# The first loads in halves, and the first norm's square sums behind the first dense products, in a single-core chain of three transformer blocks

## The chip, the cores and the metric

The kernel runs on one core of a Trainium2 chip. The metric is the device time in microseconds (us) of one execution; smaller is better. A core has TensorE (PE: matrix products; its weight loads are shown as PEld and overlap the products), ScalarE (ACT), VectorE (DVE), GpSimd (POOL) and SyncE (SP), which here only issues transfers. Each engine runs its own program in order, and the programs meet at semaphores.

## The reference

Three blocks are run one after the other on 256 tokens of 1024 numbers. Only the first lines of the first block matter here:

```python
h = rmsnorm(x, attn_norm_g)            # x * rsqrt(mean(x*x) + 1e-6) * g
m = rmsnorm(mem, mem_norm_g)
proj = h @ w_in                        # 8704 columns: da_q, da_k, da_v, wa_q, ...
da_q, da_k, da_v, wa_q, wa_k, wa_v, xa_q, gates = jnp.split(proj, offsets, axis=-1)
```

Three attentions (differential, windowed, and to a memory), their gates, an output product, a mixture of 16 experts, and then the second and third blocks follow. None of them is changed.

## The kernel before

**Layout.** Activations lie feature by feature: `self.x` is 128 partitions by 8 groups `f` of features by 256 tokens. The inputs come so from memory (`xT`, 1024 KB). `vecs` holds the gains, and the first columns of `consts` an identity matrix and a matrix of ones over 1024.

**Products in three parts.** For accuracy every dense product takes both operands as a rounded half and a rest: a = hi + lo. ScalarE writes `hi` (`a_hi`, line 582), VectorE writes `lo = a - hi` (`v_lo`, line 593), and `t_three` (lines 620, 621, 622) issues three matmuls: hi·hi, hi·lo, lo·hi. A 1024 KB load of weights holds 256 output columns of all 1024 rows; it is rounded in two pieces, `h = 0` (rows 0 to 511) and `h = 1`, each 128x1024. `t_fm` works through one such load as 24 matmuls of 256 token columns for `h = 0` and 24 for `h = 1`, and it yields after each of the two.

**The first projection.** The first stage is `mix`. The projection `daq` (4 loads, called c0 to c3 here, load numbers 0 to 3) doesn't wait for the norm: its right operand `xg` is x times the gain, in two halves (`gained` on ScalarE, line 1965; `gained_lo` on VectorE, line 1493), and the factor 1/sqrt(mean square) is applied to the product afterwards, in `q_out` (line 1508). That factor, `RSTD`, comes from this sequence: ScalarE squares x (`a_square`, line 953, four pieces), TensorE sums them over the features with the matrix of ones (`t_rms`, line 936, eight plain float32 products, shown as 16 matmul records), ScalarE takes the root (`a_sd`, line 971), VectorE the reciprocal (`v_rstd`, line 976). The same sequence, with squares added up first by GpSimd, is run for `mem` some 30 us later. The normed x proper (`v_normed`, lines 983 and 989; `a_normed`, line 966) is wanted only by the second projection, `dak`.

**Order of the programs.** There is no planner for this part: each engine's order is written out by hand.
- TensorE (`t_mix`): wait for all first inputs; `t_rms("n1")`; c0 to c3 of `daq`; then `dak`, with `t_rms("mem")` inside it.
- ScalarE (`a_mix`): four squares; gained(0); hi of load 0, h=0; gained(1); hi of load 0, h=1; gained(2); gained(3); the load of the root's table (line 804); `a_sd("n1")`; then hi of load 1, both pieces, then hi of load 2, and so on.
- VectorE (`v_mix`): gained_lo(0); lo of load 0, h=0; gained_lo(1); lo of load 0, h=1; gained_lo(2), (3); `v_rstd("n1")`; then lo of load 1, both pieces; `q_out` of c0; pieces of the normed x; lo of load 2; and so on.
- SyncE (`sync`): x (line 522), then the weight loads in order (line 544), with `mem` behind load 1 (line 546) and small tables behind load 3. ScalarE's own queue carries `vecs` and the first `consts`. Four slots hold weights, so load 4 waits until both pieces of load 0 are rounded.

The PSUM banks for `daq` are two in turn, so c2 needs `q_out` of c0 done.

Of the kernel before, what the change touches and what calls it, by code (L numbers as in the profile page):

```python
# [231 lines left out]
class Program:  # L232
    def __init__(self, nc, A, out, ctx):
# [24 lines left out]
        self.side = Landed(sem("side_landed")), Landed(sem("side2_landed"))  # L258
        self.router_in, self.tables_in = Landed(sem("router_landed")), Landed(sem("second_tables_landed"))
# [16 lines left out]
        self.first_all, self.rest_all = (self.first_in, 48), (self.rest_in, 16 * 9)  # L276
# [243 lines left out]
    def sync(self, e):  # L520
        S, A = Met(), self.A
        e.dma_start(self.B(2), A["xT"]).then_inc(*self.first_in.one())
        for q in self.order:
# [19 lines left out]
            for r, (view, src) in enumerate(load.parts):  # L543
                e.dma_start(view(base), src).then_inc(*(self.row_in[r] if q == self.tail else self.landed[load.slot]).one())
# [32 lines left out]
    def a_hi(self, e, i, h):  # L577
        load, step = self.loads[i], self.loads[i].n // 2
        c = slice(h * step, h * step + step)
        for w in self.Aw.new(load.value, *self.pair_free(i, h)):  # L580
            e.wait_ge(*w)
        e.activation(self.WH[load.pair][:, c], self.base(i)[:, c], ACT.Copy).then_inc(*self.act.inc(("hi", i, h)))  # L582
# [5 lines left out]
    def v_lo(self, e, i, h):  # L588
        load, step = self.loads[i], self.loads[i].n // 2
        c = slice(h * step, h * step + step)  # L590
        for w in self.Vw.new(load.value, self.act.val(("hi", i, h))):
# [678 lines left out]
    def t_mix(self, e):  # L1270
        DB, KB, OB = Ring(0, 1), Ring(2, 3, 4, 5, 6, 7, 0, 1), Ring(6, 7)
        H, mp, act = self.H, self.mp, self.act
        for w in self.Tw.new(self.first_all):
            e.wait_ge(*w)
        self.t_rms(e, "n1", self.B(9), KB)
        run(self.t_proj(e, "daq", 4, self.xg, self.halves("xg"), DB, self.by_dve("daq")))
# [87 lines left out]
    def a_mix(self, e):  # L1364
        act = self.act
        for j in range(4):
            self.a_square(e, "n1", self.x, self.B(9), j, [self.first_all])
        gained = lambda j: self.a_gained_hi(e, "xg", self.x, self.xg[0], lambda f: self.V("attn_norm_g", f), j, [])
        gained(0)
        self.a_hi(e, 0, 0)  # L1370
        gained(1)
        self.a_hi(e, 0, 1)
        gained(2)
        gained(3)
        self.a_sqrt_table(e)
# [107 lines left out]
    def v_mix(self, e):  # L1483
# [3 lines left out]
        for w in self.Vw.new(self.first_all):  # L1487
            e.wait_ge(*w)
        def gained_lo(j):
            for f in (2 * j, 2 * j + 1):  # L1490
                for w in self.Vw.new(self.act.val(("xg", "h", f))):
# [5 lines left out]
        gained_lo(1)  # L1497
        self.v_lo(e, 0, 1)
        self.v_next = 1
        gained_lo(2)  # L1500
# [156 lines left out]
    def g_mix(self, e):  # L1657
        for w in self.Gw.new(self.first_all):
# [1863 lines left out]
    def begin(self, dry):  # L3522
# [3 lines left out]
        for landed in (*self.landed, *self.row_in, *self.side, self.first_in, self.rest_in, self.late_in, self.rows_in, self.router_in, self.tables_in):  # L3526
# [102 lines left out]
```

## Time and the profile before

| | |
|---|---|
| time, median of 3 runs | 2701.94 us (2701.65 to 2703.44) |
| the profiled execution's own time | 2701.89 us |
| span in its profile | 2699.2 us |
| TensorE busy | 2302.2 us, 85% of the span |
| VectorE busy | 1255.6 us, 47% |
| ScalarE busy | 932.8 us, 35% |
| GpSimd busy | 54.8 us, 2% |
| moved by the DMA queues | 695.45 MB, mean 258 GB/s |

The span runs from the first to the last record of the profile; the execution's own time is 2.7 us more. Busy time is the union of an engine's instructions. The profile is of one execution.

### The profile page before, as it was taken

The numbers are of one execution on the slowest core, as the hardware profiler recorded it, in microseconds if no ns is written. First come the engines' busy times: TensorE is split into PE (matmuls) and PEld (weight loads), VectorE is DVE, ScalarE is ACT, GpSimd is POOL, SyncE is SP. The second block draws the span as 40 slices with busy tenths as digits, with TensorE's granted clock in tenths as the row PEclk, the third lists the DMA queues.
The fourth block names the chain that finished last, engine by engine and source line by source line (L and its number), as shares of the span: only waits on it lengthen the run. The fifth ranks groups of instructions, "written<-read, shape, count | busy, mean of one in ns | idle before, by whom it ended". The sixth has DMA issues, their size and how long they took to land.

```text
span 2699.2 us, 37912 instructions
## 1 busy us (share of the span) xinstructions
PE 2302.2 (85%) x16606; PEld 1676.6 (62%) x16606; DVE 1255.6 (47%) x1778; ACT 932.8 (35%) x1528; POOL 54.8 (2%) x40
## 2 busy tenths in 40 slices
PE   8999999556566556666699999999999999998998
PEld 8897785112122111212378888888888888887887
DVE  6567663001000000101287865577656556866655
ACT  6556551000000000000255654455443543743443
POOL 0000000000000000000100000000000000003000
PEclk9999999888878887878899999999999999999999
DMA  7543479999999999999934365665554654313652
GB/s 249 172 156 110 140 281 389 430 432 431 431 430 431 430 431 430 432 431 432 347 110 157 105 224 187 203 234 201 190 187 172 203 184 145 120 60 127 203 187 93
DMA packets 236549, 695.45 MB, mean 258 GB/s; under 512 B 10304, under 2 KB 189888, under 8 KB 221408
## 3 DMA queue, kind: packets, MB, share of 16 engines
q1 hardware_dynamic: 234080, 679.15, 65.9%
q0 software_dynamic: 2016, 13.67, 1.4%
q8 instruction: 130, 2.13, 0.3%
q14 instruction: 35, 0.29, 0.0%
q10 hardware_dynamic: 288, 0.22, 0.0%
HBM read 691.96 MB, written 1.05 MB: 257 GB/s over the span
## 4 chain that ended last, share of the span: by engine, by line
PE 63%; DMA 28%; DVE 6%; ACT 2%; issue 1%; SPq 0%; ACTq 0%; DVEq 0%
DMA af<-in_w_exp_up 18%; PE ps L620 16%; PE ps L622 16%; PE ps L621 16%; DMA af<-in_w_exp_down 9%; PE ps L1765 4%; PE ps L1802 2%; DVE ar L593 2%; PE ps L2771 1%; PE ps L2335 1%; ACT af L1124 1%; DVE af L1163 1%; PE ps L936 1%; PE ps L1232 1%; DVE sm L1202 0%
## 5 line engine op out<-in xcount | busy, mean ns | idle before, releaser
L620 PE MATMUL ps<-ar 128*128 128x512 f32 (+2 forms) x2648 | 926.2, 350 | 7.6 <-DVE ar L3486 2.1
L621 PE MATMUL ps<-ar 128*128 128x512 f32 (+2 forms) x2648 | 906.7, 342 | 0.8 <-issue 0.8
L622 PE MATMUL ps<-ar 128*128 128x512 f32 (+2 forms) x2648 | 907.0, 343 | 0.0
L593 DVE TENSOR_TENSOR ar<-af,ar 128x1024 fp32r<-128x1024 f32 x516 | 609.4, 1229 | 216.4 <-ACT ar L582 216.3
L582 ACT ACTIVATE ar<-af 128x1024 fp32r<-128x1024 f32 x516 | 511.8, 1048 | 130.9 <-PE ps L622 114.2
L620 PEld LDWEIGHTS ps<-ar 128*128 128x128 f32 x2648 | 502.1, 190 | 81.3 <-issue 9.6
L622 PEld LDWEIGHTS ps<-ar 128*128 128x128 f32 x2648 | 502.0, 190 | 59.2
L621 PEld LDWEIGHTS ps<-ar 128*128 128x128 f32 x2648 | 502.7, 190 | 56.4 <-issue 1.5
L1765 PE MATMUL ps<-af 128*32 128x512 f32 x2048 | 322.0, 787 | 230.3 <-DMA af<-in_w_exp_up 153.7
L1765 PEld LDWEIGHTS ps<-af 128*32 128x32 f32 x2048 | 74.9, 139 | 468.6 <-issue 189.3
L1939 DVE TENSOR_TENSOR af<-af,ps 128x512 f32<-128x512 f32 x16 | 11.0, 688 | 534.1 <-ACT af L1849 534.1
L1802 PE MATMUL ps<-af,cst 128*32 128x512 f32 x1024 | 155.6, 754 | 87.9 <-DMA af<-in_w_exp_down 76.4
L1849 ACT ACTIVATE af<-ps 128x512 f32<-128x512 f32 x16 | 9.6, 597 | 582.4 <-PE ps L1765 582.4
L1654 DVE TENSOR_TENSOR af<-ps,af 128x512 f32<-128x512 f32 x76 | 48.1, 684 | 262.9 <-PE ps L1814 249.0
L1802 PEld LDWEIGHTS ps<-af,cst 128*32 128x32 f32 x1024 | 38.8, 133 | 191.5 <-DMA af<-in_w_exp_down 101.1
L1856 ACT ACTIVATE cst<-ps 128x512 f32<-128x512 f32 x16 | 9.6, 597 | 271.1 <-PE ps L1802 271.1
L2392 DVE TENSOR_TENSOR af<-af,ps 128x256 f32<-128x256 f32 x66 | 27.5, 421 | 124.7 <-ACT af L2363 124.7
L2363 ACT ACTIVATE af<-ps 128x256 f32<-128x256 f32 x66 | 25.0, 384 | 135.1 <-PE ps L622 135.0
L1124 ACT ACTIVATE af<-af,sm 128x256 f32<-128x256 f32 (+1 forms) x136 | 64.0, 474 | 21.0 <-DVE sm L1210 13.2
L2354 ACT ACTIVATE ar<-ps 128x512 fp32r<-128x512 f32 x44 | 26.3, 599 | 80.5 <-PE ps L2335 80.5
L1112 ACT ACTIVATE af<-ps 128x384 f32<-128x384 f32 (+1 forms) x60 | 29.4, 536 | 52.8 <-PE ps L1076 52.8
L2379 DVE TENSOR_TENSOR ar<-ps,ar 128x512 fp32r<-128x512 f32 x44 | 30.4, 692 | 26.5 <-ACT ar L2354 26.3
(324 smaller groups left out, 1655.3 us busy)
## 6 DMA issues: line engine op xcount, KB each, us to landing
af<-in_w_exp_gate SPq DMA_DIRECT2D x30, 4096.0 KB, 33.5
af<-in_w_exp_up SPq DMA_DIRECT2D x30, 4096.0 KB, 33.4
af<-in_w_exp_down SPq DMA_DIRECT2D x28, 4096.0 KB, 33.6
af<-in_ffn_w_in SPq DMA_DIRECT2D x88, 1024.0 KB, 5.7
af<-in_ffn_w_out SPq DMA_DIRECT2D x44, 1024.0 KB, 5.2
af<-in_w_in SPq DMA_DIRECT2D x34, 1024.0 KB, 5.3
af<-in_sgu_w_in SPq DMA_DIRECT2D x16, 1024.0 KB, 6.9
af<-in_w_exp_down SPq DMA_DIRECT2D x7, 2048.0 KB, 12.0
```

Source lines behind the costliest of these rows:

```text
L582: e.activation(self.WH[load.pair][:, c], self.base(i)[:, c], ACT.Copy).then_inc(*self.act.inc(("hi", i, h)))
L593: e.tensor_tensor(self.WL[load.pair][:, c], self.base(i)[:, c], f_(self.WH[load.pair][:, c]), ALU.subtract).then_inc(*self.dve.inc(("lo", ...
L620: e.matmul(o, lh, rh, start=start, stop=False, skip_group_check=True)
L621: e.matmul(o, lh, rl, start=False, stop=False, skip_group_check=True)
L622: return e.matmul(o, ll, rh, start=False, stop=stop, skip_group_check=True)
L1112: e.activation(self.PT()[:, m, 0:at[1].stop], self.ps[:, 4 + m, 0:at[1].stop], ACT.Copy).then_inc(*self.act.inc((name, "p", i, m)))
L1124: e.activation(d, d, ACT.Exp, bias=st[:, g:g + 1], accum_out=st[:, 4 + g:5 + g]).then_inc(*self.act.inc((name, "e", i, g)))
L1654: e.tensor_tensor(d, it(self.bank((name, c))), d, ALU.add).then_inc(*self.dve.inc(("out", name, c)))
L1765: t = e.matmul(ps[32 * j:32 * j + 32, bb, :], XE[:, k, c:c + 32], k_(self.base(q), rows)[:, r, 512 * j:512 * j + 512], start=k == 0, stop= ...
L1802: t = e.matmul(ps[o:o + 32, b, :], self.AT_[x % 2][:, at:at + 32], k_(self.base(q), rows)[:, r, 512 * c:512 * c + 512], start=j == 0 and r ...
L2379: e.tensor_tensor(lo[:, v, :], it(self.bank((name, "t", c))), f_(hi[:, v, :]), ALU.subtract).then_inc(*dve.inc((name, "l", c)))
L2392: e.tensor_tensor(G, G, up, ALU.mult).then_inc(*done)
```

## The change

What is loaded stays the same, in more pieces. The first 1024 columns of x (feature groups 0 to 3), then the first half of load 0 (rows 0 to 511), then the rest of x, then the rest of load 0 are issued as four transfers of 512 KB in place of two of 1024 KB, each with a semaphore of its own or, for the last, the slot's. The instructions that round the first piece wait for the first halves only.

ScalarE's order becomes gained(0), hi(0, h=0), gained(1), gained(2), hi(0, h=1), gained(3), and then the four squares, the table, `a_sd`. VectorE's becomes gained_lo(0), lo(0, h=0), gained_lo(1), gained_lo(2), lo(0, h=1), gained_lo(3), and then, as before, `v_rstd`, lo of load 1. TensorE runs both halves of c0 first, then `t_rms("n1")`, then c1 to c3. No arithmetic changes.

```diff
-        self.first_all, self.rest_all = (self.first_in, 48), (self.rest_in, 16 * 9)
+        self.tables_all, self.half_all = (self.first_in, 32), ((self.x_half_in, 16), (self.w_half_in, 16))
+        self.first_all, self.rest_all = (self.tables_all, (self.x_rest_in, 16)), (self.rest_in, 16 * 9)
...
-        e.dma_start(self.B(2), A["xT"]).then_inc(*self.first_in.one())
+        e.dma_start(self.B(2)[:, 0:1024], A["xT"][:, 0:1024]).then_inc(*self.x_half_in.one())
+        (view, src), place = self.loads[0].parts[0], self.base(0)
+        e.dma_start(view(place)[:, 0:4, :], src[:, 0:4, :]).then_inc(*self.w_half_in.one())
+        e.dma_start(self.B(2)[:, 1024:2048], A["xT"][:, 1024:2048]).then_inc(*self.x_rest_in.one())
...
             for r, (view, src) in enumerate(load.parts):
+                if q == 0:
+                    e.dma_start(view(base)[:, 4:8, :], src[:, 4:8, :]).then_inc(*self.landed[load.slot].one())
+                    continue
...
-        for w in self.Aw.new(load.value, *self.pair_free(i, h)):
+        for w in self.Aw.new(self.half_all[1] if i == 0 and h == 0 else load.value, *self.pair_free(i, h)):
...
-        for w in self.Vw.new(load.value, self.act.val(("hi", i, h))):
+        for w in self.Vw.new(self.half_all[1] if i == 0 and h == 0 else load.value, self.act.val(("hi", i, h))):
...
     def t_mix(self, e):
-        for w in self.Tw.new(self.first_all):
+        daq = self.t_proj(e, "daq", 4, self.xg, self.halves("xg"), DB, self.by_dve("daq"))
+        next(daq)
+        next(daq)
+        for w in self.Tw.new(*self.first_all):
             e.wait_ge(*w)
         self.t_rms(e, "n1", self.B(9), KB)
-        run(self.t_proj(e, "daq", 4, self.xg, self.halves("xg"), DB, self.by_dve("daq")))
+        run(daq)
...
     def a_mix(self, e):
-        for j in range(4):
-            self.a_square(e, "n1", self.x, self.B(9), j, [self.first_all])
-        gained = lambda j: self.a_gained_hi(e, "xg", self.x, self.xg[0], lambda f: self.V("attn_norm_g", f), j, [])
+        gained = lambda j: self.a_gained_hi(e, "xg", self.x, self.xg[0], lambda f: self.V("attn_norm_g", f), j,
+                                            [self.tables_all, self.half_all[0]] if j < 2 else self.first_all)
         gained(0)
         self.a_hi(e, 0, 0)
         gained(1)
+        gained(2)
         self.a_hi(e, 0, 1)
-        gained(2)
         gained(3)
+        for j in range(4):
+            self.a_square(e, "n1", self.x, self.B(9), j, self.first_all)
         self.a_sqrt_table(e)
         self.a_sd(e, "n1", 1e-6)
...
         gained_lo(0)
         self.v_lo(e, 0, 0)
         gained_lo(1)
+        gained_lo(2)
         self.v_lo(e, 0, 1)
         self.v_next = 1
-        gained_lo(2)
         gained_lo(3)
         self.v_rstd(e, "n1")
```

## Rows read from the trace of the kernel before

**Rows 1.** The page, busy time: engine, us, share of the span, instructions.

```profile
PE 2302.2 (85%) x16606; PEld 1676.6 (62%) x16606; DVE 1255.6 (47%) x1778; ACT 932.8 (35%) x1528; POOL 54.8 (2%) x40
```

**Rows 2.** Busy time by stretch: us and instructions by engine, granted clock, DMA share.

```profile
0.00:300.00 300.00, 286.81 (x1879) 249.97 (x1880) 197.79 (x304) 177.82 (x339) 4.11 (x7) 0.99 0.51 169
700.00:1300.00 600.00, 362.63 (x2528) 117.97 (x2532) 46.85 (x82) 13.14 (x22) 0.00 (x0) 0.81 1.00 431
```

**Rows 3.** SP's waits over the span: us in total, times, longest.

```profile
SPq L544 <- PE ps L1765: 438.3, 47, 15.6
```

**Rows 4.** The chain that ended last, in order of time: start us, us, what.

```profile
1.25 6.01 DMA cst<-in_consts
...
8.05 6.35 PE ps L936 x16
...
43.19 0.88 PE ps L936 x4
44.09 0.48 ACT sm L971
44.60 1.77 DVE sm L976
...
48.78 1.24 DVE ar L593
```

**Rows 5.** TensorE's timeline: first matmuls of c0 and c1; start us, us.

```profile
14.05 0.47 PE L620 MATMUL ps<-ar 128*128 128x256 f32 x1
...
19.98 0.28 PE L620 MATMUL ps<-ar 128*128 128x256 f32 x1
```

**Rows 6.** Line 936 in two windows: min/median/max ns, first and last start us.

```profile
L936 PE MATMUL ps<-af,cst x3: 634/634/634, 10.7 to 11.6; 128*128 128x256 f32 x3
...
L936 PE MATMUL ps<-af,cst x5: 379/454/634, 12.4 to 13.8; 128*128 128x256 f32 x5
```

**Rows 7.** ScalarE's timeline, in order of time.

```profile
7.28 2.19 ACT L953 ACTIVATE af<-af 128x512 f32<-128x512 f32 x4 [4.26 <-DMA cst<-in_consts]
9.37 0.89 ACT L1965 ACTIVATE ar<-af,vec 128x256 fp32r<-128x256 f32 x2
10.17 1.04 ACT L582 ACTIVATE ar<-af 128x1024 fp32r<-128x1024 f32 x1
11.11 0.89 ACT L1965 ACTIVATE ar<-af,vec 128x256 fp32r<-128x256 f32 x2
...
15.97 0.46 ACT L971 ACTIVATE sm<-ps,sm 128x256 f32<-128x256 f32 x1
```

**Rows 8.** VectorE's timeline, in order of time.

```profile
16.46 1.75 DVE L976 RECIPROCAL sm<-sm 128x256 f32<-128x256 f32 x1 [0.42 <-ACT sm L971]
18.13 2.29 DVE L593 TENSOR_TENSOR ar<-af,ar 128x1024 fp32r<-128x1024 f32 x2
```

**Rows 9.** The transfer of x, issued at 0.81 us: KB, median us from issue to landing.

```profile
af<-in_xT SPq DMA_DIRECT2D x1, 1024.0 KB, 5.8
```

**Rows 10.** The first weight transfer, line 544, issued at 1.3 us.

```profile
DMA to landing us min/median/max: 8.6/8.6/8.6
```

**Rows 11.** Busy time by stretch from the start; last: clock, DMA share, GB/s.

```profile
0.00:4.20 4.20, 0.00 (x0) 0.00 (x0) 0.18 (x5) 1.28 (x1) 0.20 (x4) 1.00 0.50 148
...
0.00:5.90 5.90, 0.00 (x0) 0.00 (x0) 0.18 (x5) 1.28 (x1) 0.20 (x4) 1.00 0.63 215
...
0.00:8.80 8.80, 0.75 (x2) 0.69 (x3) 0.18 (x5) 2.81 (x4) 0.20 (x4) 1.00 0.78 264
```

**Rows 12.** TensorE's timeline at 244 us: start us, us, idle before it.

```profile
244.06 1.29 PE L1050 MATMUL ps<-cst,af 128*128 128x128 f32 x8 [2.49 <-DVE ar L1577]
```

**Rows 13.** Busy time by stretch: behind two idle stretches of TensorE.

```profile
245.50:248.90 3.40, 3.40 (x13) 2.03 (x10) 1.81 (x3) 2.75 (x5) 0.00 (x0) 0.51 0.00 0
...
2472.50:2478.00 5.50, 5.42 (x52) 4.83 (x52) 1.02 (x1) 0.00 (x0) 0.59 (x1) 1.00 0.53 183
```

**Rows 14.** TensorE's timeline at 2472 us: start us, us, idle before it.

```profile
2472.58 1.03 PE L2998 MATMUL ps<-af 64*64 64x64 f32 x29 [2.50 <-issue]
```

More of the change, by code:

```diff
@@ L258, in __init__ @@
         self.side = Landed(sem("side_landed")), Landed(sem("side2_landed"))
+        self.x_half_in, self.x_rest_in = Landed(sem("first_half_of_x_landed")), Landed(sem("second_half_of_x_landed"))
+        self.w_half_in = Landed(sem("first_half_of_weights_landed"))
         self.router_in, self.tables_in = Landed(sem("router_landed")), Landed(sem("second_tables_landed"))
@@ L1486, in v_mix @@
             e.memset(column, eps).then_inc(*dve.inc(*(["eps"] if eps == 64e-5 else [])))
-        for w in self.Vw.new(self.first_all):
-            e.wait_ge(*w)
         def gained_lo(j):
             for f in (2 * j, 2 * j + 1):
-                for w in self.Vw.new(self.act.val(("xg", "h", f))):
+                for w in self.Vw.new(*([self.tables_all, self.half_all[0]] if j < 2 else self.first_all), self.act.val(("xg", "h", f))):
                     e.wait_ge(*w)
@@ L1657, in g_mix @@
     def g_mix(self, e):
-        for w in self.Gw.new(self.first_all):
+        for w in self.Gw.new(*self.first_all):
             e.wait_ge(*w)
@@ L3525, in begin @@
             count.n, count.dry = 0, dry
-        for landed in (*self.landed, *self.row_in, *self.side, self.first_in, self.rest_in, self.late_in, self.rows_in, self.router_in, self.tables_in):
+        for landed in (*self.landed, *self.row_in, *self.side, self.first_in, self.rest_in, self.late_in, self.rows_in, self.router_in, self.tables_in, self.x_half_in, self.x_rest_in, self.w_half_in):
             landed.n = 0
```

## The prediction

> **What bounds the kernel now.** I read the page first. TensorE is busy 85% of the span, the other engines less than half [rows 1]. Busy time by stretch then splits the kernel: in the first 300 us TensorE is busy 286.8 us at a granted clock of 0.99, with the DMA engines half used; from 700 to 1300 us the DMA share is 1.00 at 431 GB/s [rows 2]. So the edited part lies in a stretch where TensorE's order is the time, and a DMA-bound stretch stands behind it. SP's waits say how the two are tied: its weight loads there wait for TensorE to give slots back (438.3 us over 47 waits) [rows 3]. A delay of TensorE at the start delays the slots, and so the stream, by the same amount.
>
> The chain that ended last shows the start: `consts` lands at 7.26, and the 16 records of line 936 follow from 8.05 for 6.35 us [rows 4]. TensorE's timeline shows c0's first dense matmul at 14.05, c1's, the 49th, at 19.98 [rows 5]. From 14 to 43 us TensorE never waits. The reader is to see one number there: TensorE's work on the norm's sums and on c0 takes 8.05 to 19.98, 11.93 us in one piece, and c1 follows at once. What happens to c1's start is the change's effect.
>
> **When c0 can start after the change.** First the transfers. The busy stretches give the bytes moved by a time (GB/s by us): 0.62 MB by 4.2, 1.27 MB by 5.9, 2.32 MB by 8.8 [rows 11]. x, vecs, consts and load 0 are 1.05 + 0.09 + 0.13 + 1.05 = 2.32 MB, so the last byte of load 0 moves at 8.8, and it lands at 1.3 + 8.6 = 9.9 [rows 10]: 1.1 us from the last byte to the semaphore. After the change, in the order of the queue: half of x and vecs (0.62 MB) land at 4.2 + 1.1 = 5.3; half of the weights with consts (1.27 MB in all) at 5.9 + 1.1 = 7.0. consts shares the engines with weight packets of its own size, so it is done about half way between, near 5.9. In the kernel before it landed at 1.25 + 6.01 = 7.26 [rows 4], later than x (0.8 + 5.8 = 6.6) [rows 9]; that is the late bound for gained(0). The rest of x I put at about 8.4, the rest of load 0 at 9.9 as now.
>
> Then the engines. gained(0) takes 0.80 us (9.37 to 10.17), one piece of hi 0.94 (10.17 to 11.11) [rows 7], one piece of lo 1.24 [rows 4]. gained(0) from 5.9 to 6.7; hi waits for the half load, 7.0 to 7.94; lo to 9.2; c0 starts at 9.2, against 14.05. Early bound 8.7, if the half load lands 0.5 us sooner; late bound 7.28 + 0.80 + 0.94 + 1.24 = 10.26, if consts lands no sooner than now. The second half of c0 doesn't wait: hi(0, h=1) runs 9.9 to 10.84, gained(3) to 11.64, gained_lo(3) is done at about 12.9, and c0's first 24 matmuls at the slow clock (below) last till 14.3. The four squares take 2.1 us (7.28 to 9.37) [rows 7] and end behind gained(3) near 13.8 and the root's table is in at about 15.1, all under c0.
>
> The Trainium skill, DMA: Bandwidth & Descriptors, section Bandwidth, advises batches of at least 1 MiB, which speaks against transfers of 512 KB. The four are queued one behind the other with full load behind them, and the 1.7 us that h=1 has to spare would cover a 10% lower rate, so the sum is the same by either.
>
> **The clock.** The norm's sums are also what TensorE warms up on. Their records take 634 ns until about 12.9 us and 379 ns behind it [rows 6], 4.85 us after the first of them; the engine had been idle since the start. So these run at the lower of the two levels (1.2 and 2.4 GHz) though the granted clock column says 1.00 there. Whatever stands first pays this: now the sums do, then c0 will. The first 4.85 us do half their work, a loss of 2.4 us in both kernels, and so I leave TensorE's 11.93 us as they are: c0 and then the sums run from 9.2 to 21.1.
>
> The Trainium skill, TensorE: Matmul & The Clock Gate, Part 1, says that "the default state is throttled, and activity releases the throttle". By that the moved sums take their warm-up away from c0; the trace agrees, in the records of line 936, and the sum already has it.
>
> **What is queued behind the moved sums.** Here is the cost. In VectorE's program lo of load 1 stands behind `v_rstd("n1")`, which waits for ScalarE's root, which waits for the sums; and hi of load 1 stands behind that root. Now the sums are done at 14.4, root 15.97, reciprocal 16.46, lo of load 1 from 18.13 [rows 7, 8]: all under c0's 5.9 us, and c1 finds its weights at 19.98. After the change c0 has been done before the sums, and nothing is left on TensorE to cover this. The price is in the trace, since `mem` runs the same sequence: sums end 44.07, root 44.09, reciprocal 44.60 to 46.37, a piece of lo 1.24 us [rows 4]. From the end of the sums: 0.02 + 0.51 + 1.77 + 1.24 + 0.05 for the hand-overs = 3.6 us. (hi of load 1 needs 0.94 us behind the root and is under the reciprocal.) TensorE stands idle from 21.1 to 24.7.
>
> The change of c1's start without anything else: 24.7 - 19.98 = 4.75 us later, which is (9.2 - 8.05) + 3.6. With the bounds of the start, 4.25 to 5.8.
>
> **The clock again.** An idle stretch of 3.6 us in a dense stage is new. The trace has two near it. Behind 2.49 us idle at 244 [rows 12] the granted clock is 0.51 from 245.5 to 248.9 [rows 13]: 3.4 us at the lower level, half of it lost, 1.7 us. Behind 2.50 us idle at 2472 [rows 14] it stays at 1.00 [rows 13]. So a shorter pause than the new one costs the clock one time in two; I take the longer one to cost it, 1.7 us (bounds 0 and 2.4, what the first ramp costs). Sum: 4.75 + 1.7 = 6.45 us.
>
> **Behind c1.** What comes later keeps its distance to c1. lo of load 2 is done about 9 us after the sums, behind `q_out` and four pieces of the normed x, and c2 wants it 3.6 + 5.9 = 9.5 us after them, later still with the slow clock. Loads 5 to 7 are issued up to 5 us later, since their slots open with lo of loads 1 to 3, but they are wanted as much later. `t_rms("mem")`, POOL's sums and `dak` shift with TensorE. I price these at nothing. If lo of load 2 ran 0.5 us late, that would be all they add.
>
> The profiled execution took 2701.89 us, 2.7 more than its span of 2699.2, and the median is 2701.94, so the sum can be added to the median: 2701.94 + 6.45 = 2708.4.
>
> **The rivals.**
> *A, the forecast:* c1 waits for the norm and the clock falls, 2708.4, chance 0.52.
> *B, the pause is there and the clock stays:* 4.75 us, 2706.7. For it: the pause at 2472. Against it: the one at 244, and 3.6 is more than 2.5. Chance 0.23.
> *C, as A, but consts lands no sooner than now:* c0 starts at 10.26, 5.8 + 1.7 = 7.5 us, 2709.4. For it: its packets may well be held up by larger ones whatever SP's pieces are. Chance 0.12.
> *D, not slower, the delay is given back:* the expert stage is bound by DMA, and if its stream began at a time that TensorE doesn't set, the 5 to 6 us would vanish there. 2701.9. It decides if the first expert loads are issued no later than now. Against it: SP waits for slots that TensorE frees [rows 3], and the shift reaches those too. Chance 0.06.
> *E, not slower, the sequence behind the sums is hidden:* if lo of load 1 were ready when the sums end, the cost would be 9.2 - 8.05, 1.15 us, 2703.1. It decides if lo of load 1 runs before the reciprocal. Against it: both programs run in order. Chance 0.04.
> *F, faster:* it would need c0 to start before 8.05 as well as E; the transfers don't allow it. All that is left, 0.03, some 2697.
>
> **How the numbers follow.** A measurement of this kernel can tell about 0.2%, 5.4 us, from no change, and 2707.3 is that bound. Of A 0.46 lies above it (an early start or a short slow stretch takes it below), all of C, and 0.04 of B: slower 0.62. The rest of A and B, D and E: 0.35 within. F: 0.03 faster. The likeliest case has its own range, with 8.7 to 10.26 for the start and 1.2 to 2.4 for the clock: 2707.4 to 2710.2. The range reaches down over B (4.25 gives 2706.2, less what a faster first ramp or a shorter hand-over might give) and up over C and 0.9 more for the ramp: 2704.5 to 2710.5. It leaves out D, E and F, 0.13, and some 0.06 above.
>
> **What the profile after would show.** First dense matmul at 9.2 (8.7 to 10.26), at the slow clock to about 14; line 936 once at full clock, 16 records in some 3.6 us, from about 17.5 to 21.1; then TensorE idle 3.6 us, released by VectorE's line 593, with lines 971 and 976 just before in the chain; c1 at 24.7; a granted clock near 0.5 for about 3.4 us in c1. c2 not waiting for line 593. The first expert load issued 6 us later. The prediction is wrong if c1 starts by 22, if lo of load 1 runs before the reciprocal, or if the delay at 100 us isn't that at the end.

## The result and the profile after

| | before | after |
|---|---|---|
| median | 2701.8 us (2699.44 to 2706.51, 8 runs) | 2710.3 us (2708.59 to 2711.68, 8 runs) |
| the profiled execution's own time | 2701.89 us | 2710.82 us |
| span in its profile | 2699.2 us | 2708.8 us |

The ratio is 1.003, 95% interval 1.002 to 1.0041: the change makes the kernel 8.5 us slower. The forecast was 2708.4, with a range of 2704.5 to 2710.5.

The page and the busy time by stretch (span stretch, its length, busy us and instructions of PE, PEld, DVE, ACT, POOL, granted clock, DMA share, GB/s) of the kernel after:

```profile
PE 2307.3 (85%) x16606; PEld 1679.1 (62%) x16606; DVE 1256.4 (46%) x1778; ACT 932.7 (34%) x1528; POOL 54.4 (2%) x40
...
0.00:300.00 300.00, 280.52 (x1842) 246.06 (x1843) 194.56 (x299) 172.17 (x325) 4.08 (x7) 0.99 0.51 165
```

No engine has more instructions than before [rows 1]. In the first 300 us TensorE is busy 6.3 us less than in [rows 2], with 37 instructions fewer: the same program is behind its old place by then. The chain that ended last (start us, us, what) shows where:

```profile
1.24 6.17 DMA cst<-in_consts
...
8.35 0.95 ACT ar L591
9.39 1.24 DVE ar L602
10.68 0.58 PE ps L629
...
19.17 3.47 PE ps L945 x16
22.66 0.48 ACT sm L980
23.17 0.97 DVE sm L985
...
24.84 1.17 DVE ar L602
```

Lines 591, 602, 629, 945, 980 and 985 are lines 582, 593, 620, 936, 971 and 976 of before. c0's first dense matmul is at 10.68 (14.05 in [rows 5]), the sums are the block at 19.17, and c1 begins at 26.05 (19.98 in [rows 5]): 6.07 us later. Between the sums and c1 stands the sequence root, reciprocal, lo, which `mem` alone had to itself in [rows 4]. In the timelines of TensorE and ScalarE (start us, us, engine, line, what, idle before it and what ended that):

```profile
26.05 0.39 PE L629 MATMUL ps<-ar 128*128 128x256 f32 x1 [3.43 <-DVE ar L602]
...
5.77 1.28 ACT L1976 ACT_TABLE_LOAD   x1 [5.77 <-DMA af<-in_xT]
7.44 0.91 ACT L1976 ACTIVATE ar<-af,vec 128x256 fp32r<-128x256 f32 x2 [0.39 <-DMA cst<-in_consts]
```

TensorE is idle for 3.43 us. What it runs at behind that, by stretch:

```profile
26.20:30.00 3.80, 3.80 (x20) 3.80 (x21) 3.80 (x9) 1.93 (x4) 0.00 (x0) 0.55 1.01 352
30.00:31.00 1.00, 1.00 (x10) 1.00 (x9) 1.00 (x1) 0.21 (x1) 0.00 (x0) 1.00 1.12 376
```

20 matmuls stand in 3.8 us at a granted clock of 0.55, the lower level, and then 10 in 1.0 us. c1's `q_out` comes 7.65 us later than before (33.60, was 25.95), so the slow stretch costs 7.65 - 6.07 = 1.58 us. An instruction that both kernels have, at 70.06 before, shows that this is the whole delay, and one near the end shows what comes on top:

```profile
77.71 0.60 ACT L916 ACTIVATE af<-ps 128x512 f32<-128x512 f32 x1 [1.65 <-PE ps L631]
...
2505.70 0.29 ACT L801 ACTIVATE sm<-sm 128x1 f32<-128x1 f32 x1 [3.75 <-DVE sm L837]
```

The second stood at 2496.11. ScalarE's instructions, matched one by one, are 7.65 us late at 70 us and 7.85 at 340 us. While the DMA engines set the pace, from 400 to 1300 us, single ones are between 6.2 and 9.3 late. From 1600 to 2300 us they are 8.1 late, and behind 2500 us 9.6 in this profile. The medians differ by 8.5.

### The profile page after: what moved, and what is told of

Read it like the earlier page. It is cut to its first block, busy times and chain, and to the rows that moved or that the text cites. A ratio compares the mean times of both kernels' runs of the same rounds, so it can differ in the third digit from the quotient of the medians.

```text
span 2708.8 us, 37916 instructions
## 1 busy us (share of the span) xinstructions
PE 2307.3 (85%) x16606; PEld 1679.1 (62%) x16606; DVE 1256.4 (46%) x1778; ACT 932.7 (34%) x1528; POOL 54.4 (2%) x40
## 4 chain that ended last, share of the span: by engine, by line
PE 62%; DMA 28%; DVE 6%; ACT 3%; issue 1%; SPq 0%; ACTq 0%; DVEq 0%
DMA af<-in_w_exp_up 18%; PE ps L629 17%; PE ps L631 16%; PE ps L630 16%; DMA af<-in_w_exp_down 9%; PE ps L1776 4%; PE ps L1813 2%; DVE ar L602 2%; PE ps L2782 1%; PE ps L2346 1%; ACT af L1133 1%; DVE af L1172 1%; PE ps L1241 1%; PE ps L945 0%; DVE sm L1211 0%
## 5 line engine op out<-in xcount | busy, mean ns | idle before, releaser
L1776 PE MATMUL ps<-af 128*32 128x512 f32 x2048 | 329.3, 803 | 231.0 <-DMA af<-in_w_exp_up 150.5
```

What stands on the lines that cost most here:

```text
L1776: t = e.matmul(ps[32 * j:32 * j + 32, bb, :], XE[:, k, c:c + 32], k_(self.base(q), rows)[:, r, 512 * j:512 * j + 512], start=k == 0, stop= ...
```

## The experiments

Every kernel is read at three places: the two instructions above ("at 70", "at 2500": how much later than in the kernel before), and matched instructions around 2300 us. Its median stands against that of the kernel before, run beside it on the same chip. One profiled execution differs from another by some us behind 2350 us (see the last section), so what happens in the first 30 us is read at 70.

| kernel | at 70 | at 2300 | at 2500 | median | of before | ratio (95%) |
|---|---|---|---|---|---|---|
| after | +7.65 | +8.1 | +9.6 | 2710.3 | 2701.8 | 1.003 (1.002 to 1.0041) |
| e1 load 1 ahead of the root | +3.07 | +3.6 | +4.25 | 2705.02 | 2702.29 | 1.0009 (0.9999 to 1.0018) |
| e2 norm behind, whole loads | +9.05 | +8.8 | +9.84 | 2711.84 | 2702.29 | 1.0035 (1.0025 to 1.0044) |
| e3 halves, norm ahead | +0.29 | +0.9 | -0.69 | 2702.43 | 2702.29 | 1.0003 (0.9994 to 1.0013) |
| e4 pause filled | +5.41 | +5.8 | +7.76 | 2708.63 | 2702.29 | 1.0021 (1.0011 to 1.003) |
| e5 start without consts | +7.45 | +7.7 | +13.2 | 2710.03 | 2702.1 | 1.0027 (1.0018 to 1.0036) |
| e6 products before c0 | +6.46 | +6.3 | +1.63 | 2703.37 | 2702.1 | 1.0003 (0.9994 to 1.0012) |
| e7 all together, x first | +1.19 | +0.1 | +1.66 | 2704.79 | 2702.1 | 1.0009 (1.0 to 1.0018) |
| e8 all together, weights first | +1.07 | +1.4 | +2.74 | 2705.5 | 2702.1 | 1.0008 (0.9999 to 1.0017) |
| e9 after, 12 small products | +7.29 | +7.2 | +2.67 | 2704.42 | 2702.12 | 1.0008 (0.9999 to 1.0017) |
| e10 before, 12 small products | -0.72 | -0.6 | -3.91 | 2696.66 | 2702.12 | 0.9979 (0.997 to 0.9988) |
| e11 before, 12 warm products | -0.72 | -0.5 | -3.56 | 2696.67 | 2702.12 | 0.9979 (0.997 to 0.9988) |
| e12 before, 24 small products | +2.97 | +3.0 | +1.08 | 2701.67 | 2702.34 | 0.9997 (0.9988 to 1.0006) |

### The two halves of the change apart: e3 and e2

**e3** keeps the four half transfers and ScalarE's squares wait by halves, but the norm stands ahead of c0 again.

```diff
     def t_mix(self, e):
-        daq = self.t_proj(...)
-        next(daq)
-        next(daq)
-        for w in self.Tw.new(*self.first_all):
+        for w in self.Tw.new(self.tables_all):
             e.wait_ge(*w)
         self.t_rms(e, "n1", self.B(9), KB)
-        run(daq)
+        run(self.t_proj(...))
     def a_mix(self, e):
+        for j in range(4):
+            self.a_square(...)
         gained(0)
...
         gained(3)
-        for j in range(4):
-            self.a_square(...)
```

> The other half of the change alone: four transfers of 512 KB, squares and sums ahead of everything as in the kernel before. Theory: the sums start near 8.2, c0 near 14.2, c1 near 20.1, no pause; time that of the kernel before within 0.1% (2701 to 2703). Rival (smaller transfers cost): c0 1 us or more later than 14.05, and a time above 2704.

TensorE's timeline of e3:

```profile
8.00 6.41 PE L945 MATMUL ps<-af,cst 128*128 128x256 f32 x16 [8.00 <-ACT af L962]
14.05 0.47 PE L629 MATMUL ps<-ar 128*128 128x256 f32 x1
```

These are the starts of before, 8.05 and 14.05 [rows 4, 5], and at 70 the delay is 0.29. While the norm stands first, landing x and load 0 in halves changes the time by nothing that the runs can tell.

**e2** does the other part alone: the norm behind c0, but x and load 0 land whole, and c0's first half waits for all of both.

```diff
-        e.dma_start(self.B(2)[:, 0:1024], A["xT"][:, 0:1024]).then_inc(*self.x_half_in.one())
-        (view, src), place = self.loads[0].parts[0], self.base(0)
-        e.dma_start(view(place)[:, 0:4, :], src[:, 0:4, :]).then_inc(*self.w_half_in.one())
-        e.dma_start(self.B(2)[:, 1024:2048], A["xT"][:, 1024:2048]).then_inc(*self.x_rest_in.one())
+        e.dma_start(self.B(2), A["xT"]).then_inc(*self.x_half_in.one())
```

> The changed kernel with x and load 0 as whole transfers of 1024 KB again; only the order of the programs is the changed one. Theory (the order alone makes the loss, and consts at about 7.3 us sets the start, not the pieces): c0 starts within 0.6 us of the changed kernel's 10.68 (load 0 lands near 9.9, and then hi 0.95 and lo 1.24 follow, so rather at 12.2 if the weights are the limit), pause of 3.4 us and fall of the clock as there; time 2710 to 2712. Rival (the halves make the loss): c1 no later than 24 us and a time of 2706 or less.

Load 0 landed at 9.82, c0 began at 12.28, and TensorE's timeline has the same pause ahead of c1:

```profile
27.46 0.39 PE L623 MATMUL ps<-ar 128*128 128x256 f32 x1 [3.43 <-DVE ar L596]
```

So the order alone costs 9.05 us at 70, and the halves take back 1.4 of them by an earlier c0. All of the slowdown is in the order.

### The pause and the clock apart: e1 and e4

**e1** leaves the norm behind c0, but moves both pieces of load 1 ahead of the root and the reciprocal.

```diff
     def a_mix(self, e):
-        self.a_sqrt_table(e)
-        self.a_sd(e, "n1", 1e-6)
         self.a_next = 1
         self.a_upto(e, 1)
+        self.a_sqrt_table(e)
+        self.a_sd(e, "n1", 1e-6)
     def v_mix(self, e):
         gained_lo(3)
+        self.v_ahead(e, self.at["daq"])
         self.v_rstd(e, "n1")
```

> The changed kernel with both pieces of load 1 rounded ahead of the root and the reciprocal, nothing else moved. Theory (the pause behind the moved sums and the clock that it costs make 5.0 of the 7.65 us): c1 starts as the sums end, near 22.7 us instead of 26.05; no pause, no fall of the granted clock; c1 is 2.7 us later than in the kernel before, and so are the first dense matmuls at 70 us; time about 2704.5. Rival (the delay comes from the smaller transfers or from later loads): c1 waits elsewhere or the delay at 70 us stays above 6 us, time 2708 or more.

TensorE's timeline of e1: the sums, c1, c2.

```profile
18.45 3.62 PE L945 MATMUL ps<-af,cst 128*128 128x256 f32 x16
21.72 0.47 PE L629 MATMUL ps<-ar 128*128 128x256 f32 x1
...
28.71 0.36 PE L629 MATMUL ps<-ar 128*128 128x256 f32 x1 [0.89 <-DVE ar L602]
```

c1 follows the sums at once and the clock stays at 1.00. The delay at 70 falls from 7.65 to 3.07. By the parts: c1 is 26.05 - 21.72 = 4.33 earlier, 1.58 of slow clock are gone, and 0.89 comes back as a wait of c2 for lo of load 2, which the root and reciprocal now hold up: 5.0 net, 4.6 measured. The forecast for e1 had not foreseen that wait: a wait that was moved away had a successor. What is left, about 3 us, is c0's later start (10.46 against 8.05 for the sums before) and the successor.

**e4** keeps the order of the changed kernel and fills the pause with seven products into a bank that nothing reads.

```diff
         self.t_rms(e, "n1", self.B(9), KB)
+        self.t_idle(e, 7, 7)
         run(daq)
```

> The changed kernel with seven idle products (ones by a table, 256 columns, into a bank that nothing reads) between the sums and c1, so that TensorE works through the 3.4 us in which c1's weights are not ready. Theory (1.6 us of the 7.65 is the clock that falls behind the pause): c1 still starts at 26.0 to 26.2, the granted clock stays at 1.00, c1 takes 5.8 us instead of about 7.4, and the delay at 70 us is 6.1 to 6.2 instead of 7.65; time about 2708.5. Rival (the clock would fall anyway, or c1 is slow for another reason): the delay at 70 us stays 7.6.

TensorE's timeline, and the stretch behind c1's start:

```profile
21.72 3.19 PE L674 MATMUL ps<-cst 128*128 128x256 f32 x14
25.32 0.39 PE L629 MATMUL ps<-ar 128*128 128x256 f32 x1 [0.41 <-DVE ar L602]
...
26.20:30.00 3.80, 3.80 (x34) 3.80 (x34) 3.80 (x9) 2.19 (x4) 0.00 (x0) 1.00 1.01 354
```

34 matmuls in the stretch in which the changed kernel has 20, at a granted clock of 1.00. c1 begins 5.34 us later than before, and at 70 the delay is 5.41: with the clock held, nothing is lost behind c1's start. The rest of the difference to the changed kernel, 7.65 - 5.41 = 2.24, is 0.73 of an earlier c1 and some 1.5 of the clock. That separates the two prices of a pause: its length, and what follows it. The 0.73 has nothing to do with the filling: c0 began at 10.37 here instead of 10.68, and it ran 0.4 us shorter. It is also why 5.41 lies below the forecast for e4, 6.1 to 6.2.

### The start of c0: e5 and e6

**e5** takes away what the profile after shows ahead of gained(0): `vecs` gets a semaphore of its own, so that gained(0) doesn't wait for `consts`, and one copy of a single column pulls ScalarE's first table load ahead of the waits.

```diff
-        e.dma_start(self.vec[:, :], A["vecs"]).then_inc(*self.first_in.one())
+        e.dma_start(self.vec[:, :], A["vecs"]).then_inc(*self.vec_in.one())
...
-                       [self.tables_all, self.half_all[0]] if j < 2 else self.first_all)
+                       [self.vec_all, self.half_all[0]] if j < 2 else [self.vec_all, (self.x_rest_in, 16)])
+        for w in self.Aw.new(self.dve.val("eps")):
+            e.wait_ge(*w)
+        e.activation(self.sm[:, 502:503], self.EPS[1e-5], ACT.Copy).then_inc(*self.act.inc())
         gained(0)
```

> The changed kernel in which the instructions that scale x wait for vecs alone (a semaphore of its own) and not for consts, and in which a one-column copy ahead of all waits brings the table load to 2 us. Theory (the first half of the weights, landed at 1.25 + 6.6 = 7.85, is next in line right behind consts): hi of load 0 from 7.85, c0 at 10.1 to 10.2 instead of 10.68, pause and clock as in the changed kernel, delay at 70 us 7.1 instead of 7.65; time about 2709.8. Rival (consts and the table alone make the start late, as the prediction's 9.2 supposed the weights to be at 7.0): c0 at 9.2 to 9.4, delay at 70 us 6.2.

ScalarE's timeline of e5:

```profile
1.73 1.28 ACT L1383 ACT_TABLE_LOAD   x1 [1.73 <-PEq L3600]
...
5.89 0.91 ACT L1980 ACTIVATE ar<-af,vec 128x256 fp32r<-128x256 f32 x2 [2.66 <-DMA vec<-in_vecs]
7.92 1.06 ACT L592 ACTIVATE ar<-af 128x1024 fp32r<-128x1024 f32 x1 [1.13 <-DMA af<-in_w_in]
```

gained(0) starts 1.55 us sooner, at 5.89, and c0 only 0.3 sooner, at about 10.4: hi now stands idle until the half load lands at 7.90. So `consts` and the table load, which head the chain of the changed kernel, had covered a transfer that was almost as late. Even the 0.3 is not clear of what profiles differ by: e1, e4 and e9 have the start of the changed kernel as it is, and their c0 begins at 10.46, 10.37 and 10.38. The delay at 70 is 7.45, 0.2 less than in the changed kernel and 0.35 more than the forecast for e5.

**e6** is the changed kernel with twelve products into an unread bank before c0, to let c0 begin at the full clock.

```diff
     def t_mix(self, e):
+        self.take(7, "warm")
+        for i in range(12):
+            for w in self.Tw.new(self.dve.val("warm")):
+                e.wait_ge(*w)
+            e.matmul(self.ps[:, 7, 0:T], self.gx[:, 0:P], self.gx[:, 0:T], start=True, stop=True)
         daq = self.t_proj(...)
     def v_mix(self, e):
+        e.memset(self.gx[:, 0:T], 1.0).then_inc(*dve.inc("warm"))
```

> The changed kernel with twelve products of ones into an unused bank from about 1.5 us on, so that TensorE has been working for 8 us when c0's weights are ready. Theory (c0's first 20 matmuls are slow only because nothing ran before them): c0 still starts near 10.7 but all its matmuls follow at 0.12 us and it ends near 16.5 instead of 19.1; sums to 20.0, the pause of 3.4 us stays, c1 near 23.5, delay at 70 us near 5.1 (3.5 if the clock doesn't fall in the pause); time about 2707. Rival (c0 is slow because of its own operands, or its second half waits for the roundings): c0 takes more than 7 us.

TensorE's timeline, and two stretches of c0:

```profile
1.26 7.36 PE L1286 MATMUL ps<-gx 128*128 128x256 f32 x24 [1.26 <-DVE sm L1505]
10.48 0.39 PE L629 MATMUL ps<-ar 128*128 128x256 f32 x1 [1.87 <-DVE ar L602]
...
10.50:11.90 1.40, 1.40 (x11) 1.40 (x12) 1.40 (x4) 1.32 (x3) 0.00 (x0) 1.00 1.10 348
11.90:16.00 4.10, 4.10 (x24) 4.10 (x23) 2.06 (x4) 4.08 (x7) 0.00 (x0) 0.58 1.05 393
```

The forecast for e6 missed: the delay at 70 is 6.46, not 5.1. TensorE had run for 7.36 us, was idle for 1.87, ran eleven matmuls at the full clock, and then fell to the lower level for about 4 us. So half of what the warming should have given did not come, and what stood between the products and the fall was a pause of 1.87 us. (e8, below, has a pause of 0.61 us at this place and no fall.) The median is 7 us below that of the changed kernel, though, with only 1.2 of them explained at 70; the rest appears behind 2350 us. That asked for e9 to e12.

### Everything that the profile suggested, at once: e7 and e8

**e7** has the warm products, e5's start, load 1 and the first piece of load 2 rounded ahead of the root, the sums behind the first half of c1, the bank ring of `daq` widened to four, and the squares of `n1` added up by GpSimd, so that TensorE sums two products for eight. Of the arithmetic only the order of that sum changes. The lines of e5 and e6 are not shown again. **e8** is e7 with the half load queued ahead of the half of x.

```diff
-        daq = self.t_proj(e, "daq", 4, self.xg, self.halves("xg"), DB, self.by_dve("daq"))
-        next(daq)
-        next(daq)
+        daq = self.t_proj(e, "daq", 4, self.xg, self.halves("xg"), Ring(0, 1, 6, 7), self.by_dve("daq"))
+        for step in range(3):
+            next(daq)
...
-        self.t_rms(e, "n1", self.B(9), KB)
+        self.t_rms(e, "n1", self.B(9), KB, (0, 1))
...
+        for name in ("n1", "mem"):
+            for j in range(1, 4):
+                self.g_sum(e, name, self.B(9), j, j == 3)
```

> What the runs so far point to, in one kernel: the start of run e5, the warming products of e6, both pieces of load 1 and the first of load 2 rounded ahead of the root, the squares of the first norm added up by GpSimd as those of mem are (two products of ones instead of eight), these two put behind the first half of c1, and four banks in turn for the first projection. Theory: c0 at 10.2 and waiting in its middle for the rounding of x's last quarter until about 13.5, c1 near 16.6, c2 near 23.3 against 25.75 in the kernel before, no pause over 1 us, the delay at 70 us is -2.4; time about 2699.5, 0.1% below the kernel before. Rival (the start costs more than the removed products give): c2 at 25.7 or later, time 2702 or more.

> Run e7 with the half of load 0 issued ahead of the half of x. Both must have landed before c0 can start, so the theory gives the same within 0.5 us: hi of load 0 starts near 7.2 instead of 7.85 but ScalarE's order puts the scaling of x first, whose half now lands near 7.8. c2 between 23.0 and 24.0, time 2699 to 2700.5. A rival would be a gain of over 1 us, from the larger piece of ScalarE's work coming first.

Both missed: +1.19 and +1.07 at 70, where e7 should have been 2.4 ahead of before, and medians of 2704.79 and 2705.5. Three things went otherwise than forecast. VectorE's and GpSimd's timelines of e7 hold one, the rounding of load 1:

```profile
13.75 4.95 POOL L956 TENSOR_TENSOR af<-af 128x512 f32<-128x512 f32 x3 [13.24 <-ACT af L963]
15.67 4.11 DVE L603 TENSOR_TENSOR ar<-af,ar 128x1024 fp32r<-128x1024 f32 x2 [1.80 <-ACT ar L592]
```

The two pieces of lo of load 1 take 4.11 us beside GpSimd's additions, 2.29 without them [rows 8]. The Trainium skill, GPSIMD Engine Reference, section Specifications, says that GpSimd's access to SBUF is shared with VectorE and contends with VectorE instructions that have two SBUF inputs; lo has two, and the trace agrees.

The second is the clock, which fell in e7's c0 behind 1.90 us idle as in e6. It did not fall in e8. There the warm products lasted longer and left TensorE idle for 0.61 us only, and all 48 matmuls of c0 stand in 5.9 us at a granted clock of 1.00. TensorE's timeline of e8, and this stretch:

```profile
10.29 0.39 PE L630 MATMUL ps<-ar 128*128 128x256 f32 x1 [0.61 <-DVE ar L603]
...
17.47 0.39 PE L630 MATMUL ps<-ar 128*128 128x256 f32 x1 [1.18 <-DVE ar L603]
...
10.30:16.20 5.90, 5.90 (x48) 5.79 (x48) 4.25 (x8) 5.90 (x10) 2.59 (x2) 1.00 1.06 380
```

c1 begins at 17.47 all the same, behind 1.18 us of waiting for lo of load 1, against 17.61 in e7. So the rounding beside GpSimd holds c1 in e8. In e7 it began 0.28 us later still (15.67, 15.39 in e8), so it would have held c1 there too, and the clock in c0 cost e7 next to nothing.

The third decides the delay at 70, and it is again a successor. c2 begins at 24.32 in e7 and 24.19 in e8, some 1.5 us ahead of before (25.75). c3 then waits for lo of load 3, in e8 as in e7 (2.37 us, until 32.48). VectorE's and TensorE's timelines of e7:

```profile
22.16 1.75 DVE L986 RECIPROCAL sm<-sm 128x256 f32<-128x256 f32 x1 [0.59 <-ACT sm L981]
...
31.33 2.35 DVE L603 TENSOR_TENSOR ar<-af,ar 128x1024 fp32r<-128x1024 f32 x2
...
32.60 0.39 PE L630 MATMUL ps<-ar 128*128 128x256 f32 x1 [2.35 <-DVE ar L603]
```

c3 began at 31.50 before, so it is 1.10 late, and that is the delay at 70 but for 0.1. Between the reciprocal and lo of load 3 VectorE works without a pause: lo of load 2, `q_out`, the pieces of the normed x. The reciprocal stood at 16.46 [rows 8]. Moving the sums and the root back moved all of this work back. Had c1 begun at the forecast 16.6, 1.0 us sooner, and the root with it, c3 would have begun near 31.6, an estimate from these rows: no sooner than before.

That e8 equals e7 within 0.2 us at 70 doesn't say what the order of the two halves is worth, since the same wait of c3 covers it.

### A gain that is not at the start: e9, e10, e11, e12

e6's median asked whether its gain came from warm products or from products at all. **e9** is the changed kernel with the twelve products 16 columns wide, **e10** the kernel before with the same, **e11** the kernel before with eleven of 256 columns and one of 16, and **e12** is e10 with 24 products. The core of e10:

```diff
     def t_mix(self, e):
+        self.take(7, "warm")
+        for i in range(12):
+            for w in self.Tw.new(self.dve.val("warm")):
+                e.wait_ge(*w)
+            e.matmul(self.ps[:, 7, 0:16], self.gx[:, 0:P], self.gx[:, 0:16], start=True, stop=True)
         for w in self.Tw.new(self.first_all):
```

> The changed kernel with twelve products of 16 columns into an unused bank at the start, done by 3 us: the same number of added instructions on TensorE as in run e6, but no warming. Run e6's delay was 6.3 us up to 2300 us and its time only 1.3 us above the kernel before; between 2350 and 2460 us, where TensorE's waits are for its own instructions, it gained 5. Theory (the place of the instructions in TensorE's stream sets those waits): the delay at 70 us is 7.6 as in the changed kernel, at 2500 us near 2.9, time about 2705.3. Rival (e6's gain late in the span came from something else, or from chance): delay about the same at 70 and at 2500 us, time 2709 to 2711.

> The kernel before with the same twelve products of 16 columns at its start. Theory of the instructions' place: nothing moves up to 2300 us (delay 0 at 70 us), and between 2350 and 2460 us about 5 us are gained, time 2697 to 2698, faster than both kernels. Rival (chance, or a gain that belongs to the changed kernel's order): 2701 to 2703.

> The kernel before with eleven products of 256 columns and one of 16, so that TensorE works from 1.3 to 8.2 us and the norm's sums run at full clock. Sums from 8.2 to 11.8 instead of 14.0; c0 waits for its weights' rest until 12.6; c1 is held until 19.3 by lo of load 1, which stands behind the root (16.0, held by ScalarE's own order), so only 0.6 of c0's 1.4 us is left: delay at 70 us -0.6. With the gain of run e10, if that is there, 0.6 below its time; without it 2701.2.

> The kernel before with twenty-four products of 16 columns at its start in place of twelve (they last from 1.3 to near 11.5 us at 0.22 us a record, so the norm's sums start some 3.5 us late, but run at full clock: sums 11.9 to 15.5, c0 1.4 us later than in the kernel before, delay at 70 us +1.4). Theory (where a block of TensorE's instructions begins decides how long it waits for them between 2350 and 2460 us, so the effect isn't in proportion to their number): the change between 2300 and 2500 us is not again -3 to -5 on top of run e10's, time 2698 to 2706. Rival (each added instruction brings the waits down): another 5 us gained there, time 2693.

TensorE's timelines of e10, e11 and e12:

```profile
1.26 5.30 PE L1277 MATMUL ps<-gx 128*128 128x16 f32 x24 [1.26 <-DVE sm L1492]
7.86 5.82 PE L936 MATMUL ps<-af,cst 128*128 128x256 f32 x16 [1.30 <-ACT af L953]
```

```profile
1.26 7.20 PE L1278 MATMUL ps<-gx 128*128 128x256 f32 x24 [1.26 <-DVE sm L1493]
8.31 3.70 PE L936 MATMUL ps<-af,cst 128*128 128x256 f32 x16
...
19.17 0.39 PE L620 MATMUL ps<-ar 128*128 128x256 f32 x1 [0.76 <-DVE ar L593]
```

```profile
1.26 10.42 PE L1277 MATMUL ps<-gx 128*128 128x16 f32 x48 [1.26 <-DVE sm L1492]
11.52 5.85 PE L936 MATMUL ps<-af,cst 128*128 128x256 f32 x16
```

In e11 the sums run at the full clock, 3.70 us for 6.35 [rows 4], and yet c1 comes only 0.8 us sooner: it now waits for lo of load 1 (19.17, behind 0.76 idle). In e10 the sums are still mostly slow (5.82 us), c1 begins at 19.28, and the reading at 70 is the same as in e11. So in the kernel before too the start is held by the rounding of load 1 within 1 us; a faster TensorE there buys no more. In e12 the small products end so late that they push the sums to 11.52, and 48 records of 16 columns left the sums at 5.85 us, so they are still mostly slow: the forecast of +1.4 for e12's delay missed (+2.97) because it took them at full clock.

e10 and e11 are the fastest kernels of the study: 2696.7 us, ratio 0.9979 (0.997 to 0.9988), faster than both. 0.6 us of the 5.5 are there at 2300 us. e9 gives the same against the changed kernel: 0.36 less at 70, and 2704.42 for 2710.3. The waits of TensorE between 2350 and 2480 us (line, what it waited for: us in total, times, longest) of the kernel before and of e10:

```profile
PE ps L2771 <- issue: 7.2, 6, 1.6
PE ps L2998 <- issue: 2.5, 1, 2.5
...
PE ps L621 <- issue: 0.8, 1, 0.8
```

```profile
PE ps L2777 <- issue: 7.7, 6, 1.9
...
PE ps L3004 <- issue: 0.4, 1, 0.4
```

"issue" is time in which TensorE waited for nothing that the profile shows but its own program. Two of these waits are gone or smaller, 2.5 + 0.8 us down to 0.4, and the six others are 0.5 longer together. That is 2.4 us of the 3.3 by which this stage is shorter in the profile (-0.6 at 2300, -3.91 at 2500); by the medians it is 4.9 (5.5 less 0.6). The rival that each product takes off a share was tried by e12: twice as many products give 3.7 us by the median (3.0 lost at 2300, 0.7 gained in all), not 10. So it is not the number of instructions ahead that counts in proportion.

What does count can be read from the traces by counting TensorE's matmul records from the first. In the kernel before, the waits of this stage stand at the records 12542, 12796, 13431, 13558, 13686, 14576, 14704, 15212 and 15596. In e10 they stand at 12542, 12796, 13686, 14068, 14576, 14704 and 15596, though 24 records were put in ahead, so that each of these numbers is another matmul of the program. In all fourteen traces each wait of this kind between 2350 and 2480 us, 112 in all, lies within about two records of 12542 plus a multiple of 127.25. So the waits come at fixed counts of TensorE's own program, and products added at the start push the program past these places by their number: the wait of 2.50 us at record 15596 [rows 14] is 0.36 at that count in e10, and in e12 it is gone, with others at 12924 and 13941. How long one of them is depends on what stands there; why was not taken apart. The profile has a queue by the name of instruction beside the data queues; in `--dma` over 2340 to 2480 us of the kernel before (packets, MB, share):

```profile
q8 instruction: 27, 0.44, 1.3%
```

These are transfers of 16 KB, 131 in the whole trace for 16606 matmul records, one for each 127. That the waits are for such a piece of the program fits; no run takes the two apart, so it is not shown. The four kernels also have one memset more on VectorE, and no run keeps it and leaves the products out.

## Why the prediction was right, point by point

**The bound** (TensorE's order is the time at the start, and the DMA-bound stretch behind it shifts as well): right. The delay at 70 us, 7.65, is 8.1 at 2300 us, behind all of the DMA-bound stretch, and the first expert load is issued 7.9 us later (376.73, was 368.87). Nothing was given back. Rival D falls. One sign of being wrong did come: the prediction wanted the delay at 100 us to be that at the end, and it is 7.65 there and 9.6 at the end of this profile (8.5 by the medians). Some 0.5 of that is added by 2300 us, and the rest is the stage behind 2350.

**The start of c0: the term that was mis-sized.** 9.2 was forecast, 10.68 measured, outside its bounds of 8.7 to 10.26. The pieces: the half load landed at 7.85 (7.0 forecast), `consts` at 7.41 (5.9; the late bound had 7.28), and a term was not in the sum at all, ScalarE's first table load. Before, it ran at 1.73 while ScalarE waited for one semaphore. Now gained(0) has two separate waits, and the table load was placed behind the first: it runs from 5.77 to 7.05. The landings of the three first pieces, for x's first half, the half load and x's rest:

```profile
DMA to landing us min/median/max: 4.9/4.9/4.9
...
DMA to landing us min/median/max: 6.6/6.6/6.6
...
DMA to landing us min/median/max: 7.4/7.4/7.4
```

Issued at 0.81, 1.25 and 1.73, they land at 5.7, 7.85 and 9.1. The forecast took bytes moved by a time from a kernel with whole transfers and added 1.1 us to each; x's half came 0.4 late, the half load 0.85. e5 says which of the three counted: with `consts` and the table load out of the way c0 moved by only 0.3 us, so the half load alone accounts for at least 1.2 of the 1.5. A row at the head of the chain names what came last, not what an experiment would gain by removing it.

**Rival C** said `consts` lands no sooner than before, c0 at 10.26 and 7.5 us in all. `consts` did land so (7.41), and 7.65 is nearly its number, but e5 shows that its mechanism decides 0.3 us. The outcome is A with a late start, by the half load.

**c0 and the sums in one piece, 11.93 us, whatever stands first:** right, and the closeness is luck. 10.68 to 22.64 is 11.96. How long the slow start lasts differs from one profile to the next: c0 alone takes 8.33 us here, between 7.90 (e4) and 8.45 (e5) in other kernels with the same c0 and nothing at the full clock ahead. The slow matmuls moved to c0 (they start 0.21 us apart until 16.17), and the sums run in 3.47 us.

**The pause, 3.6 us:** right, 3.43, with the sequence that `mem` had shown: root at 22.66, reciprocal at 23.17, lo at 24.84. e1 takes it away by order alone, e2 has it to the same 3.43 with other transfers. Rival E falls.

**The clock, 1.7 us:** right, 1.58, and e4 shows it apart from the pause. Rival B falls. That the clock would fall was a guess from one row for and one against, and more rows bear it out for this pause only: all five profiles with the 3.43 us (after, e2, e5, e6, e9) have the fall, and c1 takes 1.56 to 1.58 us longer in each. For pauses of some 2.5 us it stays open. The one at 244 [rows 12] cost the clock in the kernel before; at the same place of e7 it did not (TensorE's timeline, and the stretch behind it):

```profile
245.24 1.29 PE L1060 MATMUL ps<-cst,af 128*128 128x128 f32 x8 [2.46 <-DVE ar L1605]
...
245.00:250.00 5.00, 4.33 (x25) 3.09 (x26) 3.14 (x5) 4.86 (x12) 0.00 (x0) 1.00 0.01 3
```

e7's delay falls from 1.19 to 0.04 us there, which is why it reads +0.1 at 2300.

**Behind c1, nothing:** right within 0.5 us up to 2300. c2 didn't wait in the changed kernel. It does in e1, where the pause is gone, for 0.89 us.

**The total.** At 70: (10.68 - 8.05) + 3.43 + 0.01 of rounding + 1.58 = 7.65, against 1.15 + 3.6 + 1.7 = 6.45 forecast. The start gives +1.5, the other terms -0.3. Another 0.9 between 7.65 and the medians' 8.5 was not in the sum: 0.45 of it is there by 2300 us, and what is left is smaller than the scatter of the stage behind 2350. Where the 0.9 comes from is not shown. So the number is right with little to spare. 2710.3 lies 0.2 us below the upper end of the range and just outside the range of the likeliest case (2707.4 to 2710.2). The room at the top was there for a late `consts` and a longer ramp, and it was used up by the half load and by the 0.9. The mechanism was forecast; that the total still fell inside is partly luck.

## What to carry to other kernels

Before work is moved behind other work, ask what stands behind it in the in-order programs of the other engines: here the sums themselves were free to move, but the rounding of the next load stood behind their root and reciprocal, and 3.4 us that c0 had covered became a pause on TensorE, with 1.6 us of slow clock on top. Move the successors with it (e1 got back 4.6 us by moving the rounding of load 1), and look for the next wait: e1 found it 0.89 us long, e7 and e8 2.4 us. Here the dense stage opened slowly whatever stood first, the sums (6.35 us before, 3.47 after) or c0, so the order there bought nothing by itself.

## What the runs showed of the hardware that was not expected

**Pauses and the clock.** Idle for 1.87 us (e6) and 1.90 us (e7) behind products at the full clock, TensorE fell to the lower level some 1.3 us after it had begun again. Behind 0.41 us (e4), 0.61 us (e8) and 0.89 us (e1) the granted clock stayed at 1.00. Behind 2.49 us it fell at 244 us of the kernel before, and behind 2.46 us at the same place of e7 it stayed.

**The slow start has no fixed length.** The same warm products open e6, e7, e8 and e11, from 1.26 us on, and their records turn from 634 to 380 ns at 4.8, 4.4, 7.0 and 5.3 us.

**What ran ahead of the sums.** Behind nothing (before) they take 6.35 us, directly behind 48 records of 16 columns in 10.42 us (e12) 5.85, and directly behind 24 records in 7.20 us, all but two of them of 256 columns (e11), 3.70.

**Where the first table load runs.** With one wait ahead of the first activation it ran at 1.73, with two at 5.77, between them. Its length, 1.28 us, is the figure of the Trainium skill, ScalarE: Activation LUTs, section What ACT_TABLE_LOAD costs.

**TensorE waits for its own program, at fixed counts of it.** Between 2350 and 2480 us it stands for 10.5 us in the eight waits shown, most at small matmuls (64x64), with no other engine late. They come at multiples of some 127 matmul records, whatever was put in ahead. Twelve small products 2350 us earlier take 5 to 6 us off the time of either kernel, 24 take less than 4 off this stage, and the 27 runs of the kernel before beside e9 to e11 spread over 8 us (2698.19 to 2706.43). e5's profile gained 5.5 us of delay between 2300 and 2500, where its median has none of them. That is as large as the change under study: of two kernels that differ only at the start, read the start in the trace and not in the total.
